# First projection of a two-block transformer kernel: tokens stationary, 512 weight columns moving, results turned back in their own banks

## The reference, cut to what matters

```python
hn = rmsnorm(h, mix_norm_pre[i])
proj = hn @ w_in[i]                       # 256 x 2048 times 2048 x 3616
z, xbc, dt_raw, u = jnp.split(proj, split_at, axis=-1)   # 1024, 1536, 32, 1024 columns
xbc = jax.nn.silu(dwconv_centred(xbc, conv_w, conv_b))   # 5 taps along the tokens
dt = jax.nn.softplus(dt_raw.astype(F32).reshape(b, L, 2, SSD_HEADS) + dt_bias.astype(F32))
```

## Time and profile before

| | |
|---|---|
| median of 3 runs | 2845.07 us (2844.88 to 2847.02) |
| profiled execution | 2844.97 us |
| its span | 2843.4 us |
| TensorE busy | 2822.3 us (99%), 13785 matmul records |
| VectorE busy | 2013.7 us (71%) |
| ScalarE busy | 1355.2 us (48%) |
| GpSimd busy | 23.6 us (1%) |
| mean of the transfers | 205 GB/s |
| granted TensorE clock, mean | 0.999 |
| first to last unit of the first projection | 9.9 to 221.3 us |

### The profile page before, as it was taken

How to read it: one execution, slowest core, us unless ns; L and a number is a source line. 1 busy time by engine, 2 the same in 40 slices (tenths; PEclk the granted TensorE clock), 3 DMA queues, 4 the chain that set the end, 5 groups by cost and what they waited for, 6 DMA issues and landing times.

```text
span 2843.4 us, 35208 instructions
## 1 busy us (share of the span) xinstructions
PE 2822.3 (99%) x13785; PEld 2364.7 (83%) x13785; DVE 2013.7 (71%) x2619; ACT 1355.2 (48%) x1717; POOL 23.6 (1%) x47
## 2 busy tenths in 40 slices
PE   9999999999999999999999999999999999999999
PEld 9998888888888888788888878888878888888887
DVE  6876799999877668756547888877665565655444
ACT  5555544444444447632334666654454444444333
POOL 2000000000000000000000000000000000000000
PEclk9999999999999999999999999999999999999999
DMA  7545687877878877456646544358767777776664
GB/s 250 152 134 173 187 256 250 255 254 247 258 252 267 269 259 259 150 160 188 184 141 186 155 119 126 117 181 263 231 193 227 220 225 225 226 226 202 192 192 152
DMA packets 299955, 583.25 MB, mean 205 GB/s; under 512 B 18393, under 2 KB 18801, under 8 KB 299152
## 3 DMA queue, kind: packets, MB, share of 16 engines
q1 hardware_dynamic: 296896, 572.01, 64.8%
q0 software_dynamic: 2320, 7.96, 0.9%
q10 hardware_dynamic: 576, 1.05, 0.1%
HBM read 578.85 MB, written 2.10 MB: 204 GB/s over the span
## 4 chain that ended last, share of the span: by engine, by line
PE 94%; DVE 4%; ACT 1%; issue 1%; DMA 0%; SPq 0%; ACTq 0%; DVEq 0%
PE psum L571 22%; PE psum L574 22%; PE psum L573 22%; PE psum L646 3%; PE psum L645 3%; PE psum L644 3%; PE psum L3075 2%; PE psum L3077 2%; PE psum L3076 2%; PE psum L519 1%; PE psum L522 1%; PE psum L521 1%; PE psum L3095 1%; PE psum L599 1%; PE psum L3135 1%
## 5 line engine op out<-in xcount | busy, mean ns | idle before, releaser
L709 DVE TENSOR_TENSOR w_lo<-w_raw,w_hi 128x1024 fp32r<-128x1024 f32 x720 | 878.0, 1224 | 567.0 <-ACT w_hi L703 563.2
L703 ACT ACTIVATE w_hi<-w_raw 128x1024 fp32r<-128x1024 f32 x720 | 762.7, 1060 | 1023.1 <-PE psum L574 1014.4
L571 PE MATMUL psum<-w_hi,x_split 128*128 128x512 f32 x1912 | 750.9, 393 | 0.4 <-DVE x_split L2199 0.4
L574 PE MATMUL psum<-w_hi,x_split 128*128 128x512 f32 x1912 | 745.3, 390 | 0.0
L573 PE MATMUL psum<-w_lo,x_split 128*128 128x512 f32 x1912 | 744.9, 390 | 0.0
L574 PEld LDWEIGHTS psum<-w_hi,x_split 128*128 128x128 f32 x1912 | 359.3, 188 | 75.5
L571 PEld LDWEIGHTS psum<-w_hi,x_split 128*128 128x128 f32 x1912 | 359.3, 188 | 73.8 <-issue 0.6
L573 PEld LDWEIGHTS psum<-w_lo,x_split 128*128 128x128 f32 x1912 | 359.6, 188 | 72.9
L571 PE MATMUL psum<-w_hi,hidden_split 128*128 128x512 f32 x704 | 274.9, 390 | 0.0
L574 PE MATMUL psum<-w_hi,hidden_split 128*128 128x512 f32 x704 | 274.0, 389 | 0.0
L573 PE MATMUL psum<-w_lo,hidden_split 128*128 128x512 f32 x704 | 273.9, 389 | 0.0
(11 more groups left out here) (392 smaller groups left out, 3678.8 us busy)
## 6 DMA issues: line engine op xcount, KB each, us to landing
w_raw<-in_w_in SPq DMA_DIRECT2D x216, 512.0 KB, 3.7
w_raw<-in_w_ada SPq DMA_DIRECT2D x192, 512.0 KB, 4.8
w_raw<-in_w_ffn_up SPq DMA_DIRECT2D x176, 512.0 KB, 4.5
w_raw<-in_w_ffn_down SPq DMA_DIRECT2D x88, 512.0 KB, 5.5
w_raw<-in_w_ff_gate SPq DMA_DIRECT2D x88, 512.0 KB, 4.3
w_raw<-in_w_ff_up SPq DMA_DIRECT2D x88, 512.0 KB, 4.4
w_raw<-in_w_ff_down SPq DMA_DIRECT2D x88, 512.0 KB, 4.8
w_raw<-in_w_out SPq DMA_DIRECT2D x64, 512.0 KB, 4.8
```

The costliest lines, as they stand in the source:

```text
L571: nc.tensor.matmul(to, x_hi[:, tokens], hi, start=u == 0 and t == 0, stop=False, skip_group_check=True)
L574: mm = nc.tensor.matmul(to, x_lo[:, tokens], hi, start=False, stop=end and t == 1, skip_group_check=True)
L703: nc.scalar.activation(w_hi[:, b.slot(n)], raw[:, b.raw_slot(k)], ACT.Copy).then_inc(w_rounded, 1)
L709: nc.vector.tensor_tensor(w_lo[:, slot], raw[:, b.raw_slot(k)], r(w_hi[:, slot]), ALU.subtract).then_inc(w_split, 1)
```

## The change

A unit of the first projection becomes 12 matmuls: 128 tokens stationary, 512 weight columns moving, one PSUM bank for each half of the tokens. At the end of a group ScalarE copies the first half of the tokens to `TOK` and VectorE the second, each scaled by 1/rms, which is now one number per partition. TensorE then turns the eight blocks of 128x128 back into the group's own two banks (`turn_in`), two steps after the group's end, and from there on the channels are on partitions as before. The scalings by a row go. The convolutions, SiLUs and their users move to other steps; ScalarE takes u out of the banks (`u_copy`) and applies z's SiLU from them. The last group is turned in the output stage, and `y_stat(0)`, `y_spread(0)`, `y_norm(0)` and what hangs on them move there by some steps. The dt projection has the tokens as stationary side as well: 64 matmuls with 64 or 32 moving columns, and 1/rms is applied with the bias. One of the four buffers of the mask products moves from `TOK` to `TAB`. Parts of the diff:

```diff
-        def stream_pe(pe, name, rhs, ready=None, first=None, late=None, parted=0):
-
-            b = PHASES[name]
+        def stream_in(pe, ready, late):
+
+            b = PHASES["in"]
...
+                for c in range(2):
+                    to = PS[:, 2 * b.set(j) + c, :]
+                    for t in range(2):
+                        x_hi, x_lo = (XS[:, 2 * u + t, v, c * P:c * P + P] for v in range(2))
+                        hi, lo = w_hi[:, slot, t], w_lo[:, slot, t]
+                        nc.tensor.matmul(to, x_hi, hi, start=u == 0 and t == 0, stop=False, skip_group_check=True)
+                        nc.tensor.matmul(to, x_hi, lo, start=False, stop=False, skip_group_check=True)
+                        mm = nc.tensor.matmul(to, x_lo, hi, start=False, stop=u == 7 and t == 1,
+                                              skip_group_check=True)
+                    if u == 7 and c == 0:
+                        mm.then_inc(S("in_half"), 1)
...
+        def stream_act_in(act, late, early):
+
+            b, k = PHASES["in"], RMS.index("mix_pre")
+            for n, (j, u) in enumerate(b.units):
+                if u == 7:
+                    act.wait_ge(S("in_half"), j + 1)
+                    act.wait_ge(rms_rstd, rms_count("mix_pre"))
+                    if j > 0:
+                        act.wait_ge(S("in_turned"), j)
+                    nc.scalar.activation(TOK[:, 0], PS[:, 2 * b.set(j), :], ACT.Copy, scale=RS[:, k, 0:1]
+                                         ).then_inc(S("in_copied_act"), 1)
+                early(n)
+                hi_unit(act, b, n)
+                late(b, j, u)
...
+        def stream_dve_in(dve, late, early):
+
+            b, k = PHASES["in"], RMS.index("mix_pre")
+            for n, (j, u) in enumerate(b.units):
+                early(n)
+                if u == 7:
+                    group_used(dve, b, n)
+                    dve.wait_ge(rms_rstd, rms_count("mix_pre"))
+                    if j > 0:
+                        dve.wait_ge(S("in_turned"), j)
+                    nc.vector.tensor_scalar(TOK[:, 1], PS[:, 2 * b.set(j) + 1, :], RS[:, k, 1:2], None, ALU.mult
+                                            ).then_inc(S("in_copied_dve"), 1)
+                lo_unit(dve, b, n)
+                late(b, j, u)
...
-        TURN_AT = {(0, 0): 20, (0, 1): 21, (1, 0): 32, (1, 1): 34}
+        TURN_AT = {(0, 0): 21, (0, 1): 22, (1, 0): 32, (1, 1): 34}
...
+            def taps(j):
+
+                t0, set_ = X_TILE[j], PHASES["in"].set(j)
+                act.wait_ge(S("in_turned"), j + 1)
+                first_tap(act, lambda f: accf(set_, f), lambda f: XBC[:, t0 + f],
+                          lambda f: prm("ssd_conv_w", 24 + t0 + f), lambda f: prm("ssd_conv_b", t0 + f))
...
+            def u_copy(j):
+
+                act.wait_ge(S("in_turned"), j + 1)
+                act.wait_ge(S("u_padded"), 1)
+                act.wait_ge(evacuated, 2 + 3)
+                nc.scalar.activation(UP[:, 4 * (j - 3):4 * (j - 3) + 4, 8:8 + L], acc(PHASES["in"].set(j)), ACT.Copy
+                                     ).then_inc(evacuated, 1)
 
             def z_silu(g):
-                act.wait_ge(evacuated, 2 + 6 + g)
-                nc.scalar.activation(SZ[:, 4 * g:4 * g + 4], SZ[:, 4 * g:4 * g + 4], ACT.Silu
-                                     ).then_inc(S("z_ready"), 1)
+
+                act.wait_ge(S("in_turned"), 6 + g)
...
+                nc.scalar.activation(SZ[:, 4 * g:4 * g + 4], acc(PHASES["in"].set(5 + g)), ACT.Silu
+                                     ).then_inc(evacuated, 1)
...
-                [(8 * j + 10, conv_silu, j) for j in range(3)] +
+                [(8 * j + 9, taps, j) for j in range(3)] + [(8 * j + 12, conv_silu, j) for j in range(3)] +
+                [(8 * j + 9, u_copy, j) for j in (3, 4)] +
                 [(at + 3, decays, m) for m, at in enumerate(PAIR_AT)] +
                 [(at + 1, decays_between, m) for m, at in enumerate(PAIR_AT)] +
                 [(at + 1, pool_out, g) for g, at in enumerate(POOL_AT)] +
-                [(49, y_square, 0), (54, y_root, 0), (56, mix_hi, 1), (56, mix_hi, 2), (57, z_silu, 1)],
+                [(54, z_silu, 0), (56, mix_hi, 1), (56, mix_hi, 2), (56, y_square, 0)],
                 "in", IN_END)
-            stream_act(act, "in", in_evac, late, early=in_early)
+            stream_act_in(act, late, in_early)
...
                 if (j, u) == (0, 1):
-                    mix_hi(3)
+                    z_silu(1)
+                    y_root(0)
                 if (j, u) == (0, 3):
                     y_square(1)
+                if (j, u) == (1, 0):
+                    mix_hi(3)
...
+                k = RMS.index("mix_pre")
+                dve.wait_ge(rms_rstd, rms_count("mix_pre"))
+                for c in range(2):
+                    ch.mark(nc.vector.scalar_tensor_tensor(c32(dx)[:, c], PS[:, 5, 64 * c:64 * c + 32],
+                                                           RS[:, k, c:c + 1], SM[:, 32:64], ALU.mult, ALU.add))
+                for c in range(2):
+                    ch.wait(ch.n - 1 + c)
+                    ins = nc.vector.scalar_tensor_tensor(c32(dx)[:, c], PS[:, 5, 64 * c + 32:64 * c + 64],
+                                                         RS[:, k, c:c + 1], c32(dx)[:, c], ALU.mult, ALU.add)
+                ins.then_inc(S("dt_biased"), 1)
...
             late, tail = beside(
-                [(8 * j + 8, lambda j: conv_half(j, 1), j) for j in range(3)] +
+                [(8 * j + 10 + half, lambda a: conv_half(*a), (j, half)) for j in range(3) for half in range(2)] +
                 [(1, first_pair, 4), (1, first_pair, 5), (2, first_pair, 6), (2, first_pair, 7)] +
                 [(2, wdt_lo, None), (3, params_copy, None), (4, lambda _: rstd_dve(dve, "mix_pre"), None),
-                 (5, skip_rows, None), (6, rstd_row, None), (6, dt_scale, None), (6, lambda_sums, None), (7, dt_bias, None), (8, minus_lambda, None), (9, dt_plus_one, None), (10, d_copy, None),
-                 (10, dt_done, None), (14, acum_columns, None), (14, acum_lo, None), (14, masked_cb, 0),
-                 (16, masked_cb, 1)] +
+                 (5, skip_rows, None), (6, lambda_sums, None), (7, dt_bias, None), (8, minus_lambda, None), (9, dt_plus_one, None), (10, d_copy, None),
+                 (10, dt_done, None), (14, acum_columns, None), (14, acum_lo, None), (15, masked_cb, 0),
+                 (17, masked_cb, 1)] +
                 [(at + 1, times_dt, x) for x, at in TURN_AT.items()] +
                 [(at + 4, mix_matrix, m) for m, at in enumerate(PAIR_AT)] +
                 [(at + 2, exponents, m) for m, at in enumerate(PAIR_AT)] +
                 [(STEP_AT[4 * t + 3] + 7, y_out, t) for t in range(7)] +
-                [(at, pooled, g) for g, at in enumerate((33, 35, 41, 43))] +
-                [(48, gate_y, 0), (54, y_recip, 0), (56, mix_lo, 1), (56, z_scale, 1), (56, mix_lo, 2)],
+                [(at, pooled, g) for g, at in enumerate((34, 36, 42, 44))] +
+                [(55, gate_y, 0), (56, mix_lo, 1), (56, mix_lo, 2)],
                 "in", IN_END)
-            stream_dve(dve, "in", in_evac, late, early=lambda n: mix_lo(0) if n == IN_END - 1 else None)
+            stream_dve_in(dve, late, lambda n: mix_lo(0) if n == IN_END - 1 else None)
             tail()
 
             def out_late(j, u):
-                if (j, u) == (0, 0):
+                if (j, u) == (0, 1):
+                    y_recip(0)
+                if (j, u) == (0, 3):
                     y_norm(0)
-                if (j, u) == (0, 1):
+                if (j, u) == (1, 0):
                     mix_lo(3)
...
                 for t in range(KT):
-                    nc.tensor.matmul(PS[0:32, 4, 0:L], WDT_HI[:, t], XS[:, t, 0], start=t == 0, stop=False,
-                                     skip_group_check=True)
-                    nc.tensor.matmul(PS[0:32, 4, 0:L], WDT_HI[:, t], XS[:, t, 1], start=False, stop=False,
-                                     skip_group_check=True)
-                    mm = nc.tensor.matmul(PS[0:32, 4, 0:L], WDT_LO[:, t], XS[:, t, 0], start=False, stop=t == KT - 1,
-                                          skip_group_check=True)
-                mm.then_inc(S("dt_by_heads"), 1)
-
-            def dt_turn(_):
-                pe.wait_ge(S("dt_scaled"), 1)
-                for c in range(2):
-                    ins = nc.tensor.transpose(PS[:, 5, 32 * c:32 * c + 32], ST[0:32, c * P:c * P + P], ident[0:32, 0:32])
-                ins.then_inc(S("dt_projected"), 1)
+                    for c in range(2):
+                        x_hi, x_lo = (XS[:, t, v, c * P:c * P + P] for v in range(2))
+                        nc.tensor.matmul(PS[:, 5, 64 * c:64 * c + 64].rearrange("p (v h) -> p v h", v=2), x_hi,
+                                         WDT_SPLIT[:, :, t], start=t == 0 and c == 0, stop=False,
+                                         skip_group_check=True)
```

(26 more changed lines are left out.)

106 lines of the change are left out of this document (19 added, 87 removed).

## The result

The change makes the kernel slower: 2863.91 us (median of 6 runs, 2861.94 to 2867.16) against 2844.98 us (6 runs) before, ratio 1.0066 with a 95% interval of 1.0053 to 1.0078. The direction is as predicted. The size is not: +18.9 us where +7.8 were forecast, and 2863.9 lies above the range, which ended at 2858.

A forecast was written before the change was run, and what follows sets the result against it. TensorE was taken to set the time, with VectorE close behind. Matmuls, turning back and dt projection (-1.5 us) plus moved steps (+9.3) gave +7.8 on 2845.0: 2852.8 us, with an 8-in-10 range of 2840 to 2858.

The forecast's parts named there:

- step 3: dt projection: old matmuls and transposes removed, -6.1 us; 64 thin matmuls at 0.112 us added, +7.2; net +1.1 us.
- step 5: Moved steps: new stops 11.2 us, old stop at 102 us gone (-1.9), hand-over within 0.5; in sum +9.3 us.
- Step 1: First projection's matmuls: 1344 at 0.120 us become 672 at 0.227 us, -8.8 us.
- Steps 2 and 4: Turning back: 7 batches of transposes at 0.89 us, +6.2 us; VectorE's and ScalarE's changed work in sum: nothing.
- (a): cb_product at step 14 in the first projection: TensorE stops for 3.2 us.
- (b): x_turn at step 21 in the first projection: TensorE stops for 2.5 us.
- (c): y_product(0) at step 24 waits for times_dt: TensorE stops for 2.3 us.
- (d): Steps 28 to 31: VectorE's work outlasts TensorE's, 2.4 us of stops; at step 36 another 0.8.
- A: The moved steps have room, no new stops, old one goes: -3.4, 2841.6 us; chance 0.36 with halfway cases.
- B: Faster by over 0.2%: as A, and the dt product costs half: -7.0, 2838 us; chance 0.12.
- D: The 512-column stream is held by the remainders; excluded beforehand, since the later stages run so.
- C: Two or three further 1 us stops in the output stage: +11 to +14, 2857 us; chance 0.12.

The follow-up runs named there:

- the kernel with the room made: The changed kernel with the old dt projection, turning and convolutions one step earlier, users at their old steps, three further steps moved: 2843.6 us, ratio 0.9993.
- the mended kernel: The changed kernel with its dt matmuls in three parts and the steps of the kernel with the room made: 2845.18 us, ratio 1.0002.
- the filled stops: The changed kernel with useless 512-column matmuls, 6 before cb_product and 5 before y_product(0): 2864.52 us, ratio 1.0059.

## Why the prediction was wrong, point by point

All terms at the tenth output unit, where the changed kernel is 17.1 us late:

| term | forecast | measured | from |
|---|---|---|---|
| 1 matmuls | -8.8 | -6.9 | 56 x (2.82 - 2.943), a unit's mean in the kernel with the room made and before |
| 2 turning back | +6.2 | +6.2 | 7 x 0.88 |
| 3 dt projection at full clock | +1.1 | +0.5 to +1.4 | kernels with it in three parts, beside the same with the old one |
| 5 new stops | +11.2 | +10.6 | waits |
| 5 old stop, hand-over | -1.9 | -1.3 | gone; drawn it was 1.71, and the shift falls by 2.0 where it stood in the kernel with the room made (units 25 to 26), 0.1 of it by pace, so 1.9 is right. The wait of L560 is 0.99, 0.36 before |
| TensorE's clock | no term | +6.8 | half of 6.8 + 3.4 + 3.4 us |
| sum | +7.8 | +16.3 | with 0.9 for the third line |

0.8 us are left, about the wait of 0.97 us before unit 4 for VectorE's x_split (L508), seen as +1.06 between units 3 and 4. It comes ahead of the dt product and of the moved steps, and took 0.3, 0.5 and 0.7 us in three kernels that differ from the changed one only behind it, so it says nothing of them. With the 1.7 at 1.89 ms the whole is 18.8, against 18.6 of span.

**What failed** is a term left out, in step 3 and again in step 5: both price TensorE's work and its stops at full clock, "64 x 0.112 = +7.2 us, net +1.1" and "it stops for 3.2 us". The clock is at nothing there without a reason given: no sentence asks what it does behind 64 thin matmuls in a row, or behind a stop. It cost 6.8 of the 17.1 us, the largest part of what the sum lacks. The profile before gave no alarm, since its 48 matmuls with 32 columns stationary and 256 moving ran at 1.00. They do so in all seven kernels that have them, in an unbroken run of 5.5 us, while the falls came 3.1 to 5.1 us into the run of 64. So it is not the length of an unbroken run alone; whether the fewer moving columns or the 128 stationary ones bring the fall was not tested apart. Parting the run alone is worth 5.8 us in the kernel before (from unit 5 to 14) and 3.1 in the changed one (5 to 13). A rival "the clock falls behind the dt product" was missing, and would have been priced from the rows: remaining matmuls x 0.1 us, then 0.2 for every 512-column one in the stretch. The Trainium skill (TensorE: Matmul & The Clock Gate, HAM oscillation) names idle gaps between bursts as what brings the half rate, and gives its cost as half the time spent there. The first holds here in part: of the 17 stops of 1.9 to 4.3 us in the first projections of these kernels nine came with half clock, and the dearest fall stands in a run with no gap. The second agrees (3.1 us for 6.8, 1.5 to 1.7 for 3.4).

**Step 1** was mis-sized by 1.9 us. The pace of 0.227 is right, but 12 times it is 2.72, and a unit measured 2.82 on average; before, 24 times 0.120 is 2.88, and it measured 2.943. I took the pace of an undisturbed stretch for all units and left out their first matmuls: behind small products the first one takes 0.33 us on average in the kernel with the room made instead of 0.227, and 0.21 before instead of 0.120. That is the larger part of both surpluses (0.10 and 0.06 a unit), but explains only some 0.5 of the 1.9 us between them; the rest stays open.

**Steps 2 and 4** held. The batch is 0.88. VectorE's and ScalarE's sums did not bind: with the same work in another order, 1.4 us of waits were left in the first projection of the kernel with the room made.

**Step 5** held place by place: (a) 3.1 for 3.2, (b) 2.2 for 2.5, (c) 2.1 for 2.3, (d) 1.5 + 0.9 + 0.8 = 3.2 for 2.4 + 0.8, the old stop gone. The pieces of one queue in a fixed order could simply be added. The hand-over cost 0.6 instead of nothing, just past the 0.5 that I allowed either way. The kernel with only the moved steps shows that the stops come from the steps and not from the new loops.

**The rivals.** A and B needed that no stop comes; they are out for the change as made, and B also because the dt matmuls step by 0.112 us and not by half of it. A's sum of -3.4 can be read in the mended kernel: +2.2 at the tenth output unit, 1.7 of it half clock, with 1.4 us of stops left, the longer hand-over and the smaller gain of step 1. (The kernel with the room made is at -0.8, but has the old dt projection.) D is out: the matmuls of a unit step by 0.227. C's further stops in the output stage did not come: the shift rises by 0.9 and 1.9 behind its first two units (the last group's turning, and small products that stood at unit 54 before, where the shift falls by 2.0), and then stands.

**What stays open.** The same stop of 3.1 us before cb_product comes with half clock in two kernels and not in a third that differs only earlier; that of 2.2 before x_turn is followed by none in five kernels and by one in a sixth; the one before y_product(0) (2.1 to 4.3) came with it in all six kernels that had it. Near 242 to 262 us and at 1.88 ms the stretches come and go between kernels with equal work there. So the 3.4 us lost with the two falls at stops of the changed kernel are priced (above, by the filled stops), and the falls went when the idle time did; but what decides whether such a stop brings one is not shown. Nor is it known why the one at cb_product went when only the dt run was parted.

## What to carry to other kernels

A matmul with few moving columns is not only a bad price for itself: a long run of them took TensorE's clock down for itself and for what followed, and the same matmuls in three parts between streaming units cost 0.7 us instead of 6.4. When an edit adds such a run, or stops like the ones here (2.1 us and more), put a term for the clock in the sum and read the granted clock in the result first. When a producer comes later by a step, add up the pieces of its queue up to the user and move the user or its rivals in the queue; drawing a waiting instruction forward only passes the wait to what stands behind it.
